# Decoder step on one core: half sums of the gate stage's input formed under the output columns, and all 44 tiles by seven products

## What is computed

```
h = h + concat(attention, pooling) @ w_out            # w_out: 2048 x 2048
gate, up = split(rmsnorm(h, g_ffn) @ w_gate_up)       # 2048 x (2 x 5632)
h = h + (silu(gate) * up) @ w_down                    # 5632 x 2048
h = h + sigmoid(rmsnorm(h, g_ple) @ w_ple_gate) * (p @ w_ple_proj)
y = rmsnorm(h, g_final)
```

## Time and profile before

| what | value |
|---|---|
| median of 3 executions | 2377.03 us (2375.16 to 2378.66) |
| the profiled execution: time, span | 2378.15 us, 2376.4 us |
| PE busy | 2281.2 us, 96% of the span |
| DVE, ACT, POOL busy | 1604.4, 1062.5, 193.9 us |
| mean granted clock of PE | 0.982 of full |

### The profile page before, as it was taken

The page is one execution under the profiler, slowest core; times in us unless marked ns, Lnnn a source line. Parts: engine busy times, 40 slices in busy tenths (PEclk is TensorE's granted clock), DMA queues, the critical chain, the costliest instruction groups (busy, mean ns, idle before and its releaser), DMA issues.

```text
span 2376.4 us, 45798 instructions
## 1 busy us (share of the span) xinstructions
PE 2281.2 (96%) x18615; PEld 2231.2 (94%) x18615; DVE 1604.4 (68%) x2079; ACT 1062.5 (45%) x1595; POOL 193.9 (8%) x87
## 2 busy tenths in 40 slices
PE   7999999999999899999999999999899999979996
PEld 6988998888999899999999999999899999969995
DVE  5355555564225788888888888888677777875332
ACT  5334354453224445454445454545344444554432
POOL 0041123201221000000000000000000000121110
PEclk8999999999999999999999999999899999989998
DMA  7454565434333355454554545457956765423432
GB/s 253 133 172 146 177 199 178 150 120 143 91 89 120 112 148 169 137 166 140 157 148 140 165 127 168 132 164 245 302 155 173 226 192 165 120 76 90 107 82 72
DMA packets 487413, 359.49 MB, mean 151 GB/s; under 512 B 8321, under 2 KB 469202, under 8 KB 486649
## 3 DMA queue, kind: packets, MB, share of 16 engines
q1 hardware_dynamic: 470201, 345.15, 49.0%
q10 hardware_dynamic: 17112, 12.95, 1.7%
HBM read 301.23 MB, written 57.29 MB: 151 GB/s over the span
## 4 chain that ended last, share of the span: by engine, by line
PE 88%; DVE 5%; ACT 2%; DMA 2%; issue 2%; SPq 1%; POOL 0%; ACTq 0%; DVEq 0%; POOLq 0%
PE acc L1114 37%; PE acc L673 31%; PE scores L1114 14%; PE scores L673 2%; PE mail_bank L673 1%; PE o_bank L673 1%; DVE w_low L1791 1%; DVE w_low L2272 1%; ACT w_high L1274 1%; DMA raw<-in_w_ple_gate 1%; DMA region<-in_x_prompt 1%; SPq L612 0%; DVE raw L2276 0%; PE mail_bank L836 0%; DMA raw<-in_w_down 0%
## 5 line engine op out<-in xcount | busy, mean ns | idle before, releaser
L673 PE MATMUL acc<-x_high,w_high 128*128 128x260 f32 x2240 | 472.1, 291 | 15.4 <-DVE w_low L1791 7.2
L673 PE MATMUL acc<-x_low,w_high 128*128 128x260 f32 x2240 | 456.2, 284 | 0.0
L673 PE MATMUL acc<-x_high,w_low 128*128 128x260 f32 x2240 | 455.9, 284 | 0.0
L1114 PE MATMUL acc<-x_high,w_high 128*128 128x260 f32 x1512 | 428.4, 283 | 12.3 <-DVE w_low L2272 11.2
L1114 PE MATMUL acc<-x_low,w_high 128*128 128x260 f32 x1512 | 427.5, 283 | 0.0
L1114 PE MATMUL acc<-x_high,w_low 128*128 128x260 f32 x1512 | 427.2, 283 | 0.0
L673 PEld LDWEIGHTS acc<-x_high,w_high 128*128 128x128 f32 x2240 | 348.7, 191 | 38.7 <-issue 27.8
L673 PEld LDWEIGHTS acc<-x_low,w_high 128*128 128x128 f32 x2240 | 349.8, 190 | 0.0
L673 PEld LDWEIGHTS acc<-x_high,w_low 128*128 128x128 f32 x2240 | 349.4, 190 | 0.0
L2272 DVE TENSOR_TENSOR w_low<-key_pages,w_high 128x1024 fp32r<-128x1024 f32 (+4 forms) x238 | 268.3, 1127 | 116.1 <-ACT w_high L1608 115.2
L2272 DVE TENSOR_TENSOR w_low<-raw,w_high 128x1024 fp32r<-128x1024 f32 (+4 forms) x245 | 274.9, 1129 | 87.2 <-ACT w_high L1608 86.1
(11 more groups left out here) (290 smaller groups left out, 3985.1 us busy)
## 6 DMA issues: line engine op xcount, KB each, us to landing
raw<-in_w_gate_up SPq DMA_DIRECT2D x48, 1024.0 KB, 6.0
key_pages<-in_w_gate_up SPq DMA_DIRECT2D x40, 1024.0 KB, 8.1
raw<-in_w_in SPq DMA_DIRECT2D x32, 1024.0 KB, 7.2
act_high_rows<-late_rounded SPq DMA_DIRECT2D x22, 910.0 KB, 5.4
act_low_rows<-late_rounded SPq DMA_DIRECT2D x22, 910.0 KB, 7.1
key_pages<-in_cache_k SPq DMA_DIRECT2D x32, 512.0 KB, 5.6
late<-in_cache_v SPq DMA_DIRECT2D x32, 512.0 KB, 6.0
raw<-in_w_out SPq DMA_DIRECT2D x16, 1024.0 KB, 5.8
```

The lines of the kernel that those rows point to most:

```text
L673: return pe.matmul(o, l, r, start=start, stop=stop)
L1114: return pe.matmul(bank, w, x, start=start and first, stop=last, skip_group_check=True)
```

## The change

1. Output columns are taken in the order of tiles 0, 8, 1, 9, ... 7, 15 (`tile_of`), so tiles k and 8 + k are ready together; `late` is loaded back by quarters to suit. Beneath columns 7 to 13 ACT and DVE form half sums 0 to 6 (`FORMED`). The column loops of ACT and DVE are written out.
2. The plain pairs are gone: `NS` is 44, so tiles 0 to 2 take seven products too. The first pair has a hand-written order on ACT and DVE (`entry`) instead of `window(0, ...)`. It runs beneath and behind column 15, whose matmuls count up `out_read` tile by tile so that `x_high` can be overwritten behind them. PE waits inside the first pair per tile (`needs`).
3. `stats(1)` sits between products S2 and A12 of the first pair, in other banks (`mail_bank`, `o_bank`); the root comes after product S3's copy, the reciprocal last in `entry`.
4. SP: weights of pair 0 in `raw` behind columns 12 and 13; pair 1 into `key_pages` once the scratch is read; the spill of `h` behind it.
5. With 44 pairs instead of 41 the parities swap: the last down visit (n = 71) is odd and uses `key_pages`. The first two slabs of `w_ple_gate` are loaded before p, one visit earlier; p waits for the end of the last visit.

```diff
-STD = 3
-NS = FF - STD
+NS = FF
+FORMED = {7: 0, 8: 1, 9: 2, 10: 3, 11: 4, 12: 5, 13: 6}
+def tile_of(column):
+    return column // 2 + HK * (column % 2)
...
# SP
             for i in (0, 1):
-                sp.wait_ge(S["w_low_done"], FFN_N + 5 + i)
+                sp.wait_ge(S["w_low_done"], FFN_N - 1 + i)
...
-            store_act(0, 4)
-            sp.wait_ge(S["t4_low"], 3)
+            sp.wait_ge(S["t_low"], 3 * (HK - 1))
+            sp.wait_ge(S["t4_low"], 2)
             load_pair(1, True)
+            sp.wait_ge(S["acc_free"], FFN_T)
+            sp.dma_start(h_spill[:, KEPT:], late[:, KEPT:]).then_inc(S["h_saved"], 16)
...
             sp.wait_ge(S["part_low"], 7 * (ALL - 1))
+            for s in (0, 1):
+                load(Slab(PLE_N + s), w_pg_v[:, :, s * P:(s + 1) * P])
+            sp.wait_ge(S["part_low"], 7 * ALL)
             sp.dma_start(p_nat, ...)
             sp.dma_start(ps_nat, ...)
             load_wp(0)
-            sp.wait_ge(S["part_low"], 7 * ALL)
...
# PE, first pair
+                        elif i == A12:
+                            stats(1)
                         elif i == A22:
                             pe.wait_ge(S["t4_low"], 3)
+                    def needs(i, k):
+                        if i == A11:
+                            pe.wait_ge(S["x_low"], KD + k + 1)
+                        elif i == S1 and k in (0, HK - 1):
+                            pe.wait_ge(S["t_low"], 3 * k + 1 if k else 3 * (HK - 1))
+                        elif i in (S2, S3) and k == 0:
+                            pe.wait_ge(S["t_low"], 3 * (HK - 1) + (2 if i == S2 else 3))
+                        elif i == A12:
+                            pe.wait_ge(S["x_low"], KD + HK + k + 1)
...
# DVE
+            for c in range(KD - 2):
+                if c == HK:
+                    dve.wait_ge(h_loaded[1], 16)
+                out_step(c)
+                if c in FORMED:
+                    t_sums(FORMED[c])
+                    t_lows(FORMED[c])
...
+            def entry():
+                raw11, raw12, raw21, raw22 = raws(0)
+                k, b2 = HK - 1, b_rows(HK - 1)[1]
+                dve.wait_ge(raw_landed[1], 16 * (BASE + 1))
+                add_sum(raw21, raw21, raw22, ALU.add, HK)
+                out_step(KD - 2)
+                part(0, A11, raw11, HK)
+                ...
+                add_sum(raw11, raw21, raw11, ALU.subtract, HK)
+                part(0, S1, raw21, HK)
+                for i in range(HK):
+                    x_low_half(i)
+                part(0, S2, raw11, HK)
+                t4_low(0, xl[:, 0:4, HT:T], t4_rows[:, 0:4, :], xh[:, 0:4, HT:T])
+                out_step(KD - 1)
+                t4_low(1, xl[:, 4:7, HT:T], t4_rows[:, 4:7, :], xh[:, 4:7, HT:T])
+                x_low_rows(HK)
+                t_sums(k)
+                t_lows(k)
+                ...
+                add_sum(raw21, raw22, raw11, ALU.subtract, HK)
+                x_low_rows(HK + 1)
+                part(0, A12, raw12, HK)
+                x_low_rows(*range(HK + 2, KD))
+                ...
+                add_sum(raw12, raw12, raw11, ALU.subtract, HK)
+                part(0, S3, raw21, HK)
+                t4_low(2, xl[:, k, HT:T], b2[:, 0:HT], xh[:, k, HT:T])
+                part(0, S4, raw12, HK)
+                part(0, A22, raw22, HK)
+                invert_root(1)
+                V.wait()
+
+            entry()
+            dve.wait_ge(S["h_saved"], 16)
+            window(1, 1, 1)
```

More of the change, by code:

```diff
@@ L1097, in _, with half_product @@
             whole(Slab(OUT_N + 1, 2), acc[1], OUT_T + 5)
-            with pe.Fori(3, KD // 2) as j:
+            with pe.Fori(3, KD // 2 - 1) as j:
                 out_pair(j)
[L1103 to L1107, removed]
+            whole(Slab(FFN_N - 2), acc[0], FFN_T - 2)
+            slab = Slab(FFN_N - 1)
+            begin(slab, FFN_T - 1)
+            for k in range(KD - 1):
+                part_of(slab, acc[1], FFN_T - 1, (k,)).then_inc(S["out_read"], 1)
+            part_of(slab, acc[1], FFN_T - 1, (KD - 1,))
+            def half_product(s, i, bank, start=False, at_tiles=range(HK), needs=None):
                 pe.wait_ge(S["part_low"], 7 * s + i + 1)
@@ L1195, in _ @@
             pe.wait_ge(S["naturals_copied"], 3)
[L1196 to L1209, removed]
+            for n in (0, 1):
+                ffn_pair(n, n)
+            with pe.Fori(1, NS // 2) as j:
+                ffn_pair(2 * j, 0)
+                ffn_pair(2 * j + 1, 1)
             for v in range(4):
-                visit(0, 1 - v % 2, NS + v)
+                visit(0, v % 2, NS + v)
             for b in range(1, BLOCKS):
@@ L1546, in norm_high, with t_scale @@
                     x_high(k, gain)
[L1547 to L1559, removed]
+            def t_scale(k, *which):
+                if 2 <= k < HK - 1:
                     act.wait_ge(S["t_low"], 3 * (k - 1))
-                for row, tile in ((b1_row, k), (b2_row, HK + k)):
-                    act.activation(row[k % 2], h_all[:, tile, :], ACT.Copy,
+                for a in which:
+                    tile = k + HK * a
+                    act.activation(b_rows(k)[a], h_all[:, tile, :], ACT.Copy,
@@ L1581, in gate, with t_highs @@
[L1581 to L1585, removed]
-            def cell_high(a, b, count, sums_ready):
+            def t_highs(k):
+                b1, b2 = b_rows(k)
+                for n, (a, src) in enumerate(((1, b1[:, HT:T]), (2, b1[:, 0:HT]), (0, b2[:, HT:T]))):
+                    act.wait_ge(S["t_summed"], 4 * k + (3 if n else 2))
+                    act.activation(xt_h[:, a, k, :], src, ACT.Copy).then_inc(S["t_high"], 1)
@@ L1640, in window @@
                 part(n, A12, raw12, q)
-                if outputs and not first:
+                if outputs:
                     act.wait_ge(S["joined"], 6 * n - 1)
@@ L2237, in cell_sum, with new_sum @@
+            def new_sum(t, step):
+                b11, b12, b21, b22, t2, t3, t4 = (cells(act_cell, n, n + 1) for n in range(7))
+                t1 = b12
                 if step == 0:
```

452 lines of the change are left out of this document (207 added, 245 removed).

## The result

The changed kernel takes 2354.65 us (median of 4 runs, 2352.12 to 2356.76) against 2377.85 for the kernel before beside it: ratio 0.9904, interval 0.9891 to 0.9917. Its profiled execution took 2355.11 us with a span of 2353.3, 23.1 less than before, nearly all of it between column 15 and the per-layer gate.

The account below looks back on a forecast made before the run. PE, busy 96% of the span, was taken as the bound. 2378.15 less 19.6 at the gate stage's start and 4.9 at the per-layer gate gave 2353.7, stated as 2354; own range 2351 to 2357, chance 0.50.

Parts of the forecast that it names:

- wait before pair 1, and at its S2: Start of pair 1: PE waits for DVE's reciprocal and the window queued behind it, 1.5 us, then 0.5 more.
- POOL on DVE's chain: First pair: POOL's addition of column 15's squares delays DVE's packed part by up to 1.28 us, taken in full.
- fall of the clock: First pair: no drop of PE's clock behind waits of at most 2.0 us; 4.6 us kept as the other end.
- four pairs: End of column 15 to end of fourth pair: 80.6 plus `stats` 0.9 and waits 5.6, 87.1 instead of 106.7 us.
- price of the half sums without cover: Output columns 7 to 13: half sums hidden beneath the columns cost 0; without that cover 7 x 3.0 = 21 us.
- Rival 1: Gate stage's start: handovers in DVE's chain cost more and the clock falls twice; 2358 to 2361 us; chance 0.18.
- Rival 2: Per-layer gate: p, issued 10 us later, comes late; gain there 0 to 2, 2357 to 2359 us; chance 0.10.
- Rival 3: First pair: POOL holds DVE up less than counted or not at all; 2348 to 2351 us; chance 0.14.
- Rival 4: Gate stage's start: `h_saved` or pair 1's data come late, little gain; 2373 to 2380 us; chance 0.03.
- Rival 5: The 43 pairs after the first: DVE never catches up, slower; 2388 us at d = 0.8 per window; chance 0.05.
- The down stage: Start of the down stage: order of loads and stores kept, cost 0, with a shift of 2 us either way possible.
- The slabs: Per-layer gate: `w_ple_gate` slabs issued earlier, so DVE's last additions end at 2119.7 instead of 2124.6; gain 4.9 us.

Follow-up runs that it names:

- e8: The changed kernel measured once more, unedited, with a profile of its own; 2355.72 us, ratio 0.991 against the kernel before.
- e3: Changed kernel with the squares of column 15 added by PE in `stats` instead of POOL; 2353.24 us, ratio 0.9895 against the kernel before.
- e2: Changed kernel with ACT taking the root before the copy of product S3, not behind; 2352.13 us, ratio 0.989 against the kernel before.
- e7: Changed kernel with 72 matmuls whose result nobody reads added behind pair 1; 2361.9 us, ratio 0.9937 against the kernel before.
- e1: Changed kernel with half sums 0 to 6 formed in one piece after column 13; 2373.04 us, ratio 0.998 against the kernel before.
- e4: Changed kernel with the first two `w_ple_gate` slabs waiting for the last visit's operands, still ahead of p; 2360.32 us, ratio 0.9929.
- e5: Changed kernel with DVE's last two additions to `h` ahead of the first `w_ple_gate` slab's low part; 2354.67 us (median of three), ratio 0.9908.
- e6: Changed kernel with the edits of e2, e3 and e5 together; 2349.39 us, ratio 0.9879 against the kernel before.

## Why the prediction was right, step by step

The time was foretold as 2354 and is 2354.65. So close a hit is in part luck: the same kernel took 2355.72 in e8, and for the profiled execution 2353.7 were foretold and 2355.11 measured. What stands is the terms, with u = 0 at the end of column 14:

| term | predicted | measured |
|---|---|---|
| start of S3 | u = 27.2 | 27.0 (752.53 - 725.58); 27.0 in e8 |
| wait before S3 | 2.0 | 1.69; 1.11 without POOL (e3) |
| end of pair 0 | u = 35.9 | 37.2; 35.8 in e8, without the fall of the clock |
| wait before pair 1, and at its S2 | 1.5 + 0.5 | 1.73 + 0.17; none with the root early (e2) |
| POOL on DVE's chain | up to 1.28 | 1.0 (e3) |
| fall of the clock | 0, bound 4.6 | 1.40 here, 0 in e8 |
| four pairs | 87.1 | 88.5 here; 87.3 in e8 |
| wait before `turn_p` | 4.2 | 4.19 |
| 72 matmuls | 8.6 | 8.7 (e7) |
| delays at S1's last tile, S2, and in A12 | 0.3, 0, 1.3 | 0.3, 0.4, 0.6; none without POOL (e3) |
| price of the half sums without cover | 21 | 17.1 by the profile, 17.3 to 18.4 by the time (e1) |

- **Where the 18.2 came from.** The matmuls give 8.6, the waits 11.3 - 3.6 = 7.7, slower matmuls behind the long waits 4.6 - 1.65 = 2.9 (1.65, since the 4.6 too was counted against the usual pace). That is 19.2; what is left over besides (`stats` and edges, 1.6 before) has grown by 1.0. It lies in short delays that the list of waits leaves out. A matmul usually starts 0.12 behind the one before it; these three, of the changed kernel, start 0.32, 0.41 and 0.33 behind (742.24, 742.91 and 749.88), for want of half sums (S1's last tile, S2's first) and of an `x_low` row (A12's last tile):

```profile
742.56 0.39 PE L1130 MATMUL scores<-half_sums_high,w_high 128*128 128x260 f32 x1
...
743.32 0.39 PE L1130 MATMUL acc<-half_sums_high,w_high 128*128 128x260 f32 x1
...
750.21 0.39 PE L1130 MATMUL acc<-x_high,w_high 128*128 128x260 f32 x1
```

  From end to end S1 takes 3.21 us, S2 3.28 and A12 3.48; in e3, without POOL's addition, each takes 2.9. That is 1.3 in all, where I had put 0.3 + 1.3.
- **The cover was the hinge**, as said, but my 7 x 3.0 = 21 was wrong in both factors: a step is 3.27, and six steps move, not seven. Of their 19.6 DVE's wait for the weights takes off 2.1, so `entry` slides by 17.5, and 17.1 of it reach the end of the fourth pair.
- **POOL and DVE.** Shown by e3 for the one sum. Beneath column 13 the changed kernel shows both directions (DVE, then POOL, in order of time):

```profile
704.48 2.29 DVE L1823 TENSOR_TENSOR w_low<-raw,w_high 128x2048 fp32r<-128x2048 f32 x1 [1.25 <-ACT w_high L1293]
706.69 1.54 DVE L2202 TENSOR_TENSOR key_pages<-key_pages 128x260 f32<-128x260 f32 x1
```

```profile
705.05 2.89 POOL L2506 TENSOR_TENSOR sums<-sums 128x520 f32<-128x520 f32 x1 [8.65 <-ACT sums L1304]
```

  POOL's addition begins within DVE's low part and takes 2.89 instead of 1.28; DVE's next sum begins within POOL's and takes 1.54 instead of 0.43. If each waits for the other to end, the ends come out: 706.77 + 1.28 = 708.05, near POOL's end at 707.94, and 707.94 + 0.35 (a sum, from start to start) = 708.29, near the sum's end at 708.23. The Trainium skill (SBUF — State Buffer, "SBUF: two separate sides") calls the port pair that both use an exclusive lock for a whole instruction; these rows agree with it.
- **The clock** is the mis-sized term. I took no fall behind the 2.0 us wait, with 4.6 as the other end. One of seven profiles with a wait of 1.69 or 1.70 at this place (that of the changed kernel, e1, e2, e4, e5, e7, e8) shows it, at 1.40 us; the other six have a clock of 1.00. That is the difference between the 87.1 foretold and the 88.5 of the changed kernel's own profile. Behind 3.5 and 5.6 us the kernel before had it both times, behind 12.45 us e1 did. Why it fell once and not six times with the same wait is open; nothing in the rows beside it differs that I could find.
- **Rival 1** (more stalls and two falls): one fall in one profile, the stalls as counted. **Rival 2** (p late): false here, though close where the slabs are late (e4). **Rival 3** (POOL costs nothing): false, 1.0. **Rival 4** (the spill late): the spill landed 15.8 us after its issue at 741.04, not the 8.8 of the earlier trace rows, so at u = 31, where I had put 28; `window(1)` began at u = 36, with no wait for a DMA. It cost nothing, with 5 us in hand, but of these e2 leaves 2.1 and e6 1.1: it is the next thing that would hold pair 1. **Rival 5** (DVE never catches up): false, its window is 18.23 in a pair of 20.15, as before.
- **The down stage** opens with waits of 2.42, 0.81 and 8.59 us, 11.8 in all, against 9.71 and four shorter ones, 12.2 before. Cost 0, as taken; where the wait falls has moved.
- **The slabs.** 4.9 foretold, 4.9 measured on the wait; when e4 takes it back, 5.0 on the wait and 4.6 to 5.7 by the time.

## What to carry to other kernels

Work that has to precede a stage belongs under the last matmuls of the stage before it, and what that is worth is the slide of the next stage's first operand (17.5 us here), not the sum of the work moved. At the handover write out both helpers' queues instruction by instruction and look for the one that sits early by habit: a root behind a copy (2.0 us), an addition on a third engine that holds the chain's engine up (1.0 us), a low part ahead of two short additions (1.8 us in e5, 2.6 in e6). Moving such a step shifts part of the wait to the next consumer of what was pushed back, as in e5, where one wait lost 2.7 and the next gained 0.8.

## What was not expected of the hardware

- The same wait of PE, 1.69 us, brought the clock to 0.50 in one profile of seven and left it at 1.00 in six. The loss was 1.40 us, a little less than the wait itself.
- SP itself was held when it issued behind two slabs: 4.34 us for the issue of p in e4, 0.37 in the changed kernel. The issue of the spill behind two slabs took 4.19 us, and it landed after 15.8; in the kernel before the issue took 0.34, and it landed after 8.8.
